# A hybrid decoder step on one core: mixers and attention of all blocks first, then the feed-forward stage over three wide blocks, each gate and up tile as seven half-depth products of sums

## The reference

```python
hp = hp + hybrid_mixer(rmsnorm(hp, g_mix), ...)        # gated conv and mLSTM heads, chunked
hp = hp + cross_attn(rmsnorm(hp, g_cross), pk, pv, w_xq, w_xo)   # 256 memory tokens, 4 heads
hp = hp + swiglu(rmsnorm(hp, g_ffn), w_gu, w_down)

def swiglu(xn, w_gu, w_down):
    g, u = jnp.split(xn @ w_gu, 2, axis=-1)
    return (jax.nn.silu(g) * u) @ w_down

y = rmsnorm(hp, g_final)                               # the same for the 8 sample tokens hs
```

## Time and profile before

| | us |
|---|---|
| runs | 2899.67, 2899.18, 2897.5; median 2899.18 |
| span of the profiled execution, first to last instruction | 2896.7 |
| the own time of that execution | not given apart; the lowest and highest run are 0.8 and 3.0 above the span |
| PE busy | 2856.6 (99%) |
| PE weight loads busy | 2694.2 (93%) |
| VectorE (DVE) busy | 1189.9 (41%) |
| ScalarE (ACT) busy | 753.1 (26%) |
| GpSimd (POOL) busy | 431.2 (15%) |
| DMA, mean of the 16 engines' traffic | 277 GB/s |

### The profile page before, as it was taken

One profiled execution on the slowest core, in us unless ns is written; L12 is line 12 of the kernel. 1 busy time (PEld: TensorE's weight loads), 2 busy tenths in 40 slices (PEclk: granted clock), 3 DMA queues, 4 the chain that ended last, 5 costly groups with the idle time before them and its releaser, 6 DMA issues.

```text
span 2896.7 us, 38358 instructions
## 1 busy us (share of the span) xinstructions
PE 2856.6 (99%) x15739; PEld 2694.2 (93%) x15739; DVE 1189.9 (41%) x2258; ACT 753.1 (26%) x1467; POOL 431.2 (15%) x284
## 2 busy tenths in 40 slices
PE   8899999999999999999999999999999999999998
PEld 7788888888899999999999999999999999999998
DVE  7735655323533344233334547434332242442123
ACT  5443343232332220113222110322211023221001
POOL 2643444444310000001000102000000000000000
PEclk9999999999999999999999999999999999999999
DMA  7887778788685788768687889967567777666675
GB/s 265 317 342 279 290 259 293 291 287 310 242 305 207 268 305 303 267 240 328 224 301 289 318 322 398 359 240 260 213 234 274 262 263 281 224 246 248 255 267 186
DMA packets 144998, 801.14 MB, mean 277 GB/s; under 512 B 15949, under 2 KB 31693, under 8 KB 65081
## 3 DMA queue, kind: packets, MB, share of 16 engines
q1 hardware_dynamic: 119216, 719.10, 67.1%
q0 software_dynamic: 16208, 67.87, 6.7%
q10 hardware_dynamic: 9400, 11.72, 1.2%
HBM read 650.30 MB, written 148.33 MB: 276 GB/s over the span
## 4 chain that ended last, share of the span: by engine, by line
PE 93%; DMA 3%; DVE 3%; issue 1%; ACT 1%; ACTq 0%; POOL 0%; SPq 0%; DVEq 0%; POOLq 0%
PE gb L628 82%; PE gb L872 3%; PE ta L872 2%; PE td L872 1%; DMA big<-kd_d 1%; DMA w_hl<-split_d 1%; PE ta L738 0%; DVE act_lo L1427 0%; DMA big<-rows_d 0%; DVE xn_lo L1398 0%; DMA made_d<-big 0%; DVE big L1392 0%; PE gm L854 0%; DMA w_raw<-w_kv 0%; PE ta L736 0%
## 5 line engine op out<-in xcount | busy, mean ns | idle before, releaser
L628 PE MATMUL gb<-xn_hi,w_hl 128*128 128x384 f32 (+2 forms) x5800 | 1581.9, 349 | 5.1 <-DVE big L1434 1.9
L628 PEld LDWEIGHTS gb<-xn_hi,w_hl 128*128 128x128 f32 x5800 | 1060.5, 188 | 53.6 <-issue 3.3
L628 PE MATMUL gb<-xn_lo,w_hl 128*128 128x384 f32 (+2 forms) x2920 | 1011.2, 346 | 0.0
L628 PE MATMUL gb<-act_hi,w_hl 128*128 128x384 f32 (+3 forms) x3184 | 846.4, 345 | 13.0 <-DVE w_hl L1403 10.9
L628 PEld LDWEIGHTS gb<-act_hi,w_hl 128*128 128x128 f32 x3184 | 579.3, 188 | 42.0 <-DVE w_hl L1403 11.2
L628 PEld LDWEIGHTS gb<-xn_lo,w_hl 128*128 128x128 f32 x2920 | 548.5, 188 | 24.0 <-issue 0.5
L628 PE MATMUL gb<-act_lo,w_hl 128*128 128x384 f32 (+3 forms) x1592 | 546.8, 343 | 0.0
L498 POOL TENSOR_TENSOR w_hl<-w_raw,w_hl 128x1024 fp32r<-128x1024 f32 x136 | 335.6, 2477 | 427.1 <-ACT w_hl L1019 427.0
L1454 DVE TENSOR_TENSOR work<-gb,r_res 128x384 f32<-128x384 f32 (+2 forms) x220 | 128.4, 586 | 581.8 <-PE gb L628 548.6
L628 PEld LDWEIGHTS gb<-act_lo,w_hl 128*128 128x128 f32 x1592 | 300.0, 188 | 12.2 <-issue 0.2
L1645 DVE TENSOR_TENSOR x<-x,gb 128x384 f32<-128x384 f32 (+2 forms) x200 | 115.6, 582 | 397.5 <-PE gb L628 394.0
(11 more groups left out here) (316 smaller groups left out, 2148.5 us busy)
## 6 DMA issues: line engine op xcount, KB each, us to landing
w_hl<-split_d SPq DMA_DIRECT2D x484, 1024.0 KB, 5.0
split_d<-w_hl SPq DMA_DIRECT2D x121, 1024.0 KB, 5.1
w_raw<-w_st SPq DMA_DIRECT2D x105, 512.0 KB, 6.3
w_raw<-w_kv SPq DMA_DIRECT2D x32, 512.0 KB, 5.5
made_d<-big ACTq DMA_DIRECT2D x32, 256.0 KB, 4.5
w_raw<-made_d SPq DMA_DIRECT2D x16, 512.0 KB, 8.0
big<-kd_d POOLq DMA_DIRECT2D x8, 1024.0 KB, 12.9
big<-vd_d POOLq DMA_DIRECT2D x8, 1024.0 KB, 12.8
```

The lines of the kernel that those rows point to most:

```text
L628: mm = pe.matmul(bank[:, 0:wd], a[:, s, k * P:(k + 1) * P], r[:, k, 0:wd], start=(first and k == ks[0] and i == 0), stop=(last and k == ks ...
```

## The change

**The order of the stages.** Mixer, projection and attention now run for all five blocks, one after the other (`G_BLK` ends after the attention output). The result x of a block is stored to DRAM (`x_d`), scaled by gain and norm (`scale_x` on VectorE, `scale_tile` for the last block), and stored again (`xn_d`), all inside the next block's mixer. Then the feed-forward stage runs over three blocks of 688, 684 and 684 tokens, the 8 sample tokens among them, which are read back from `xn_d`. Squares and scaling for the next block's norm now stand in the attention stage. SP issues these transfers and the gate rows; GpSimd issues none of them.

**The products.** The two halves of the depth and the two halves of the tokens make a 2x2 matrix B of activations; gate and up tile times depth halves make a 2x2 matrix A of weights. Instead of eight products of a gate and up pair, seven are made of sums of these parts, each 4 depth tiles of 128 by 344 or 342 columns. Their results are added up in PSUM, where several products share a bank, and by VectorE. The weight sums and their splits are made on the core for every block anew (nothing is stored split), the four activation sums once per block. Hidden tiles come in groups of 4, 4, 4, 2, 4 and 4.

```diff
-FFG = [8, 7, 7]
+FT0 = [0, 688, 1372]
+FW = [688, 684, 684]
+FH = [w // 2 for w in FW]
+FFG = [4, 4, 4, 2, 4, 4]
+PRODUCTS = 7
+NU = 8
+NQ = 4
+LOOK = 5
+T_B11, T_B21, T_T4, T_B22, T_T1, T_T2, T_T3 = range(7)
+OPERAND = [T_B11, T_B21, T_T2, T_T1, T_T3, T_B22, T_T4]
...
+def pooled(u):
+    _, _, f, p = UNITS[u]
+    return f < 0 or p in (0, 6)
...
+        def unit_source(u):
+            _, gr, f, p = UNITS[u]
+            q = ENTRY[u]
+            if f < 0:
+                return raw_tile(q)[:, 0:FFG[gr] * P]
+            if p == 3:
+                return s1w[:, PAIR[u] % 2, :]
+            side, part = ((0, 0), (0, 1), (0, 0), None, (1, 0), (0, 1), (1, 1))[p]
+            return raw_tile(q + side)[:, part * 512:part * 512 + 512]
```

PE in a pair and in the down tiles of a group:

```diff
+                for p, bank in enumerate((gate, low, gate, high, gate, high, gate)):
+                    u = unit_at(b, gr, f, p)
+                    if p == 2:
+                        pe.wait_ge(copied, 3 * j + 1)
+                    elif p == 4:
+                        pe.wait_ge(copied, 3 * j + 2)
+                    elif p == 5:
+                        pe.wait_ge(copied, 3 * j + 3)
+                    elif p == 6:
+                        pe.wait_ge(c22_done, j + 1)
+                    unit_ready(u)
+                    if first:
+                        pe.wait_ge(t_lo, 7 * b + p + 1)
+                    t = OPERAND[p]
+                    for k in range(4):
+                        for i, (a, r) in enumerate(((0, 0), (0, 1), (1, 0))):
+                            mm = pe.matmul(bank[:, 0:n], units[:, u % NU, a, k * P:(k + 1) * P], tq[:, t, r, k, 0:n],
...
+            for b in range(NFB):
+                for gr, size in enumerate(FFG):
+                    for f in range(size):
+                        pair(b, gr, f)
...
+                    for m in range(2):
+                        unit_ready(unit_at(b, gr, -1, m))
+                        down(b, gr, m, range(size - 1), size)
+                    pe.wait_ge(ah_lo, j + size)
+                    for m in range(2):
+                        down(b, gr, m, (size - 1,), size)
+                    for m in range(2, KT):
+                        unit_ready(unit_at(b, gr, -1, m))
+                        pe.wait_ge(evac_done, d + 2 * (m - 1))
+                        down(b, gr, m, range(size), size)
+            sum_final(NFB - 1)
```

ScalarE rounds each weight unit five units ahead (`unit_high(u + LOOK)`), copies three products out of PSUM (p = 0, 2, 3), applies silu twice and rounds the hidden tile. GpSimd makes the remainders of units p = 0 and 6 and of all down tiles. VectorE does the rest:

```diff
+            def weight_sum(j, i):
...
+                if i == 0:
+                    raw_ready(v, q)
+                    raw_ready(v, q + 1)
+                    a = v.tensor_tensor(s1, up[:, 0:512], up[:, 512:1024], ALU.add)
+                elif i == 1:
+                    a = v.tensor_tensor(up[:, 0:512], gate[:, 0:512], up[:, 0:512], ALU.subtract)
+                elif i == 2:
+                    v.wait_ge(unit_lo_p, LOW_P[u])
...
+                    a = v.tensor_tensor(gate[:, 0:512], s1, gate[:, 0:512], ALU.subtract)
+                else:
...
+                    a = v.tensor_tensor(gate[:, 512:1024], gate[:, 512:1024], gate[:, 0:512], ALU.subtract)
...
+            for u, (b, gr, f, p) in enumerate(UNITS):
+                if f >= 0:
+                    pair_step(u, b, gr, f, p)
+                else:
+                    if p == 0:
+                        hidden_low(b, pair_of(b, gr, FFG[gr] - 1), FFG[gr] - 1)
+                    evacuate(b, gr, p)
+                    if gr == NG - 1:
+                        if 2 <= p:
+                            square_sum(b, p - 1)
+                        if b < NFB - 1:
+                            for i in {4: (0, 1), 5: (2, 3)}.get(p, ()):
+                                made_operand(b + 1, i)
+                            for i in {6: (0, 1), 7: (2, 3)}.get(p, ()):
+                                operand_low(b + 1, i)
+                if gr == 0 and f == 0 and p < 3:
+                    operand_low(b, p + 4)
+                for ahead, i in ((6, 0), (5, 1), (4, 2), (2, 3)):
+                    if u + ahead < len(UNITS) and UNITS[u + ahead][2] >= 0 and UNITS[u + ahead][3] == 0:
+                        weight_sum(PAIR[u + ahead], i)
+                if u + LOOK - 1 < len(UNITS) and not pooled(u + LOOK - 1):
+                    unit_low(u + LOOK - 1)
```

```diff
-DM, DO, DX = 1, 2, 3
+DM, DO, DX = 1, 2, 4
...
+            def fold(src, n, out):
+                while n > 2:
+                    n //= 2
+                    st(pool.tensor_tensor(src[..., 0:n], src[..., 0:n], src[..., n:2 * n], ALU.add))
+                    st.settle()
+                st(pool.tensor_tensor(out, src[..., 0], src[..., 1], ALU.add))
+                st.settle()
...
+            def piece(i):
...
+                    st(pool.tensor_tensor(part, part, row.rearrange("p (o d) -> p o d", o=1).to_broadcast([P, MT, 512]), ALU.mult))
+                    st.settle()
+                    fold(part.rearrange("p m (h d) -> p m h d", h=2), 256, ds[:, :, t, 2 * j:2 * j + 2])
```

1372 lines of the change are left out of this document (830 added, 542 removed).

## The result

| | before | after |
|---|---|---|
| median of the runs, us | 2898.3 (2897.0 to 2899.7) | 2921.9 (2919.5 to 2929.1) |
| ratio, 95% interval | 1 | 1.0087 (1.0073 to 1.0102) |
| span of the profiled execution | 2896.7 | 2917.6 |
| mean granted clock | 0.997 | 0.985 |

The change makes the kernel slower by 0.87%, 23.5 us. The forecast was 2867, 1.1% faster; the time lies inside the range that was given, but on the other side of no change.

What follows compares the result with a forecast made beforehand. PE was taken to set the pace at full clock. From 2896.7 us: -66 feed-forward stage, +25 decode, +3 next norm, +6 tail gave 2864.7, with 2.5 of median over span 2867 us; range 2815 to 2925.

Steps and rivals of the forecast that it cites:

- matmuls of the feed-forward stage: Feed-forward stage: 8712 matmuls at 156.7 and 155.8 ns cost 1360 us, 115 under the 1475 of before.
- what the stage takes beyond them: PE's waits at entry, block changes, groups of two pairs, sums and odd gaps: together 49 us (15 to 86).
- decode work beside the mixers: Mixers two to five: VectorE meets GpSimd's decode work at about nine heads' ends, +25 us (0 to 48).
- next norm in the attention: Next block's norm moves into the attention; three first tiles wait for scales and remainders, +3 us (0 to 10).
- tail: End of the kernel: scales of 688 columns, a larger store and two more sums, +6 us (4 to 8).
- Steady pairs: Feed-forward gate and up pairs: VectorE's 9.6 us and the other engines' work fit PE's 13.2 us, costing nothing.
- The changes of block: Two changes of feed-forward block: VectorE ends late and operands come late, 12 us each, 24 (10 to 40).
- The groups of two pairs: Once per block, down tiles too short to cover the last hidden remainder: 3 us each, 10 (3 to 18).
- Six slots, 25 us of weights, cover that: SP's queue: waiting up to 8 us for gate rows, weight tiles queued behind, is covered by weights already loaded.
- decode too late: Rival, chance 0.10: PE waits for scores and values in attention and last mixer output; 2933 us at 12 us a piece.
- VectorE as the bound: Rival, chance 0.08: in feed-forward pairs VectorE takes 13.9 us, over 66 pairs 46 us more, 2913 us.
- nearly all hidden: Rival, chance 0.30: feed-forward waits only 25 us and mixers 5, as VectorE keeps up and GpSimd slips between; 2820 us.

Runs made afterwards that it cites:

- e2: Changed kernel, but in each block's first group ScalarE copies the last hidden tile before it rounds the fifth down unit: 2905.1 us, ratio 1.0031.
- e1: Changed kernel, but the gate rows of the first block go through GpSimd's queue again: 2912.0 us, ratio 1.0053.
- e12: e9 with the sum over ones back where the changed kernel has it and the decode output products in tile 5 and later in tile 7: 2862.7 us, ratio 0.9884.
- e9: Changed kernel with e1, e2, e3, earlier operand work at block changes, later decode products and sum over ones, earlier squares in first scores: 2870.5 us, ratio 0.9905.
- e3: Changed kernel, but the transposes of a head's result stand later in PE's order in the mixers: 2911.3 us, ratio 1.0055.
- e6: Changed kernel without GpSimd's arithmetic for the 32 cache pieces, all transfers kept: 2919.2 us, ratio 1.0071.
- e11: Kernel before the change, with PE made to wait for GpSimd at eleven places of the last feed-forward stage, longer than in e8: 2986.2 us of span.
- e8: Kernel before the change, with eleven shorter stalls of PE in the last feed-forward stage; only three waits over 0.4 us came, no total given.

## Why the prediction was wrong

The median lies 55 us over the forecast: 13 in the stage, 33.5 ahead of it, 6 in the tail, and 2 because it lies further over the profiled span than before. Where a row of the table is a time lost, half clock is counted in it.

| term | foreseen | measured |
|---|---|---|
| matmuls of the feed-forward stage | 1360 | 1374 |
| what the stage takes beyond them | 49 | 48 |
| decode work beside the mixers | 25 | 19 |
| next norm in the attention | 3 | about 8 |
| gate rows on SP | 0 | about 12 |
| pitch of the matmuls that read xn | 0 | about 15 |
| wait ahead of the stage's first product | within the 49 | 4 |
| tail | 6 | 12 |

Ahead of the stage 19 + 8 + 12 + 15 + 4 are 58 of the 61.5 lost. A mixer start that is 3 us earlier works against it, and the other 6 or so are small: a wait of 2.5 us at the end of the third mixer with its half clock, and the decode step's normalisation.

**The matmuls** were right in kind: the pitch followed the columns, and the unbroken pieces of a pair show it, 13.11 us for 84 or 156.1 ns at 342 columns, against 155.8 from the line. At 344 it is 158.1 for 156.7. A group's down tiles take 159 to 159.5 a matmul, of which 157.0 to 157.4 is pitch and the rest short breaks, some 0.4 us a group. Over 8712 matmuls that is 14 us, the whole miss of this term, and about half of it is pitch. No weight load held the pitch. The Trainium skill (TensorE: Matmul & The Clock Gate, Back-to-back issue gap) gives N/2.4 + 2.5 ns for the isolated gap between warm matmuls; an estimate from it for 342 columns is 145.0 ns, and the trace, with a weight load for every matmul, disagrees.

**Steady pairs** cost nothing, as foreseen; VectorE is busy for 9.3 us of 13.1 (9.6 was the sum). This is one pair:

```profile
2071.21:2084.32 13.11, 13.11 (x86) 13.11 (x85) 9.27 (x15) 6.88 (x13) 2.58 (x2) 1.00 0.12 41
```

**The waits of the stage** came out at the foreseen sum, 1422.3 - 1373.9 = 48.4, partly by chance. The entry's first pairs cost 5.6 us and the wait ahead of them 3.6, for 7. The changes of block were named rightly, VectorE full and operands late. Behind a change the four pairs of the first group take 59.3 us where 52.45 are matmuls; ahead of it the last group's down tiles take 34.4, the wait included, where others take 30.6: 10.6 us each, clock and all, for 12. The groups of two pairs cost 1.3 each, for 3. In the place of what they left stand the first down tiles of each block, 17.8 us in all with their half clock (36.3 to 36.9 against 30.5 to 30.7), which e2 removed. That wait was not foreseen; that it filled what the others left free of the 49 is luck. "Six slots, 25 us of weights, cover that" counted slots, and looked only at PE as the one who waits. ScalarE was the one, with another tile's work behind it.

**The step that failed** is that same sentence, the price of nothing for SP. It asked how long the weights are covered, not who waits for what is moved. The gate rows of the first block had been on GpSimd's queue. On SP's they stand behind weight tiles and are asked for at 162 us; e1 gave 9.9 us back. With e2 that makes 26 of the 55 us between 2867 and 2922. A second price of nothing, the pitch of the matmuls that stayed as they were, was off by some 15 us: the prediction took 173.4 and 226.7 ns as given wherever the columns were the same. Why matmuls that read xn became slower, no run shows.

**Decode on GpSimd** was right in mechanism and near in size: seven waits of 15.4 us and two half-clock stretches, about 19 for 25. Of the nine heads foreseen seven showed a wait, one of them of 0.3 us; at the head that was shown the slack of 0.7 us was used up by two instructions (L2151 and L2155) and not by six. A piece takes 8.3 us, where 5.8 to 7 was the estimate and 8.0 the limit that the rival gave for the values; its folds take 4.6 us and not the 2.5 foreseen. The values were in time all the same, in e12 too: the rival's margin had been put too tight.

**Next norm** cost 7.8 us in the first scores alone (a 4.1 us wait, its half clock, the sum's own matmuls, and 1.3 of xn's pitch) and 1.5 or so in a later block, of which 1.0 is again the pitch: about 8 without it, in place of 3 in all. e9 shows the cause of the first to be ScalarE's order: its squares stood behind weight tiles whose slots PE had to free.

**The tail** was 12 us for 6: the last sum over ones waits 2.8 us for a square and then runs at half clock, and the scales take 6.8 us.

**The missing term** is the clock. Every wait was priced at its length. Twelve more stretches of half clock cost an estimated 21 to 22 us, about what the span grew by. The kernel before had few such stretches, but it could have warned: its two waits of over 2.3 us after the start (2.54 us at 86.3, 2.55 at 112.9) were each followed by one.

The rivals: decode too late and VectorE as the bound did not decide, and the waits were not nearly all hidden. The matmuls did get cheaper, 80 us less of PE's busy time in the stage. No rival had the mechanisms that decided, and that the measured time lies within the range is no credit to the sum.

## What to carry to other kernels

When a transfer moves to another queue, list for it when it becomes ready, when its new place in the queue is reached and who waits for it; a queue's free slots say nothing about the last. When an in-order engine prepares work far ahead, put what the bound engine needs next in front of what it needs later. One edit of each kind, e1 and e2, was worth 26 us here. Price a PE wait of over some 2.3 us at its length and, as it mostly came here, 1.4 to 2.8 us more, and prefer several short ones; measure the pitch of the matmuls that you did not touch as well; and when an edit removes a wait, look at once for what is late next, which gave back a third of e3 and most of e6.

## What was not expected of the hardware

At half clock the fixed part of the pitch is gone. Two pieces of PE's timeline in e11, at clock 1.00 and at 0.50:

```profile
2613.05 0.33 PE L643 MATMUL gb<-xn_lo,w_hl 128*128 128x384 f32 x1
2613.23 0.51 PE L643 MATMUL gb<-xn_hi,w_hl 128*128 128x384 f32 x2
2613.57 0.33 PE L643 MATMUL gb<-xn_lo,w_hl 128*128 128x384 f32 x1
...
2846.61 0.52 PE L643 MATMUL gb<-xn_lo,w_hl 128*128 128x384 f32 x1
2846.93 0.84 PE L643 MATMUL gb<-xn_hi,w_hl 128*128 128x384 f32 x2
2847.57 0.52 PE L643 MATMUL gb<-xn_lo,w_hl 128*128 128x384 f32 x1
```

Three matmuls take 0.52 us at full clock, 173.3 ns each: 160.0 for 384 columns at 2.4 GHz and 13.3 more. At half clock they take 0.96 us, 320.0 ns each, exactly 384 columns at 1.2 GHz. So half clock costs a factor of 1.85 and not 2 (e8's theory had 346 ns), and whatever the 13.3 ns are, they do not add to the columns at the slower clock.

Cache transfers whose consumer does no work any more made PE wait for other transfers (e6), 8.0 us in two waits. And the pitch of matmuls of one shape, in one kernel, with the same weights, differs by the tensor that they read (176.6 and 173.3 ns at 384 columns), also where that tensor is the stationary operand (234 ns at 512 columns, 227 before); neither the start address to 128 bytes nor GpSimd's arithmetic nor the rate of DMA traffic explains it.
